# Sums of squares for queries and keys as two rounded passes, with the rotary products later in VectorE's order

## What is computed

```python
h = rms_norm(x, norm_w[i])
proj = jnp.einsum('bld,dn->bln', h, w_in)
# A: 4 heads of 128 with two softmax maps each, B: 4 query and 2 key heads,
# C: 4 latent heads (low-rank query and key), D: pooling; each times SiLU(gate)
q = rms_norm(q_raw, q_norm_w)      # over 64 or 128 numbers of a head
k = rms_norm(k_raw, k_norm_w)
q, k = rotate(q), rotate(k)        # part of A's, all of B's, 64 of C's
p = softmax(q @ k.T * scale)
y = p @ v
x = x + concat(A, B, C, D) @ w_out[i]
```

## Time and profile before

| | |
|---|---|
| median of three runs | 905.96 us (905.85 to 906.21) |
| the profiled execution | 905.9 us, its span 904.1 us |
| TensorE matmul busy | 896.1 us, 99% |
| VectorE busy | 639.3 us, 71% |
| ScalarE busy | 566.3 us, 63% |
| TensorE clock granted | 1.000 of full speed (2.4 GHz) |

### The profile page before, as it was taken

One profiled execution on the slowest core, in us unless ns is written; L12 is line 12 of the kernel. 1 busy time (PEld: TensorE's weight loads), 2 busy tenths in 40 slices (PEclk: granted clock), 3 DMA queues, 4 the chain that ended last, 5 costly groups with the idle time before them and its releaser, 6 DMA issues.

```text
span 904.1 us, 18068 instructions
## 1 busy us (share of the span) xinstructions
PE 896.1 (99%) x7070; PEld 860.1 (95%) x7070; DVE 639.3 (71%) x1073; ACT 566.3 (63%) x985; POOL 0.2 (0%) x4
## 2 busy tenths in 40 slices
PE   8999999999999999999999999999999999999998
PEld 7999998998999999999999999999999999999998
DVE  7785987779777776766665659876787667766552
ACT  7678756577666667745554588556676666665331
POOL 0000000000000000000000000000000000000000
PEclk9999999999999999999999999999999999999999
DMA  8754433333434343444455553344324444445562
GB/s 333 264 197 142 150 129 131 123 139 113 149 138 146 134 156 121 154 144 188 169 199 186 187 181 146 126 136 160 140 98 183 140 141 159 150 159 187 187 211 70
DMA packets 22996, 143.83 MB, mean 159 GB/s; under 512 B 2560, under 2 KB 4736, under 8 KB 6528
## 3 DMA queue, kind: packets, MB, share of 16 engines
q1 hardware_dynamic: 22768, 142.64, 43.7%
q10 hardware_dynamic: 144, 0.04, 0.0%
HBM read 140.58 MB, written 2.10 MB: 158 GB/s over the span
## 4 chain that ended last, share of the span: by engine, by line
PE 94%; ACT 3%; DVE 2%; DMA 1%; issue 0%; SPq 0%; ACTq 0%; DVEq 0%
PE dense L733 26%; PE dense L735 25%; PE dense L734 25%; PE s_ps L902 4%; PE o_ps L938 4%; PE norm_ps L857 2%; PE t_ps L917 2%; ACT w_hi L1028 1%; DVE w_lo L1331 1%; DMA x<-xt_dram 1%; PE swap_ps L881 0%; ACT h_hi L1009 0%; PE swap_ps L735 0%; PE norm_ps L735 0%; PE norm_ps L734 0%
## 5 line engine op out<-in xcount | busy, mean ns | idle before, releaser
L733 PE MATMUL dense<-h_hi,w_hi 128*128 128x272 f32 (+2 forms) x1440 | 427.2, 297 | 1.9 <-DVE h_lo L1311 1.8
L735 PE MATMUL dense<-h_hi,w_lo 128*128 128x272 f32 (+2 forms) x1440 | 412.8, 287 | 0.0
L734 PE MATMUL dense<-h_lo,w_hi 128*128 128x272 f32 (+2 forms) x1440 | 411.0, 285 | 0.0
L1331 DVE TENSOR_TENSOR w_lo<-raw,w_hi 128x1024 fp32r<-128x1024 f32 (+1 forms) x257 | 313.3, 1219 | 87.3 <-ACT w_hi L1028 80.5
L1028 ACT ACTIVATE w_hi<-raw 128x1024 fp32r<-128x1024 f32 (+1 forms) x257 | 271.4, 1056 | 70.8 <-PE dense L735 56.1
L733 PEld LDWEIGHTS dense<-h_hi,w_hi 128*128 128x128 f32 x1440 | 271.4, 188 | 7.4 <-issue 3.0
L734 PEld LDWEIGHTS dense<-h_lo,w_hi 128*128 128x128 f32 x1440 | 271.5, 189 | 1.2
L735 PEld LDWEIGHTS dense<-h_hi,w_lo 128*128 128x128 f32 x1440 | 271.2, 188 | 0.0
L733 PE MATMUL dense<-y_hi,w_hi 128*128 128x272 f32 (+1 forms) x500 | 143.6, 287 | 0.5 <-DVE w_lo L1331 0.3
L735 PE MATMUL dense<-y_hi,w_lo 128*128 128x272 f32 (+1 forms) x500 | 142.7, 285 | 0.0
L734 PE MATMUL dense<-y_lo,w_hi 128*128 128x272 f32 (+1 forms) x500 | 142.4, 285 | 0.0
(11 more groups left out here) (173 smaller groups left out, 805.7 us busy)
## 6 DMA issues: line engine op xcount, KB each, us to landing
raw<-w_stream_dram SPq DMA_DIRECT2D x128, 1024.0 KB, 4.8
out_dram<-x SPq DMA_DIRECT2D x8, 256.0 KB, 5.9
x<-xt_dram SPq DMA_DIRECT2D x3, 544.0 KB, 8.9
raw<-w_stream_dram SPq DMA_DIRECT2D x3, 512.0 KB, 7.6
con<-consts_dram SPq DMA_DIRECT2D x1, 984.0 KB, 8.2
x<-xt_dram SPq DMA_DIRECT2D x2, 272.0 KB, 4.8
raw<-w_stream_dram SPq DMA_DIRECT2D x2, 256.0 KB, 4.5
d_w<-consts_dram SPq DMA_DIRECT2D x2, 256.0 KB, 5.5
```

What stands on the lines that cost most here:

```text
L733: nc.tensor.matmul(ps, whi, xhi, start=first, stop=False)
L734: nc.tensor.matmul(ps, whi, xlo, start=False, stop=False)
L735: return nc.tensor.matmul(ps, wlo, xhi, start=False, stop=last)
L1331: signal(nc.vector.tensor_tensor(w_lo[:, g % RING, 0:n], raw[:, e % RAW, CHUNK * half:CHUNK * half + n], w_hi[:, g % RING, 0:n].bitcast(F3 ...
```

## The change

All 36 sums of squares of queries and keys are made by two passes of fp32r operands instead of one product of float32 operands. The squares are split into a high part `sq_hi` and a low part `sq_lo`. For a single tile ScalarE writes the high part with a rounding copy after the square, and a new stage `sq_low` on VectorE subtracts. For a pair VectorE makes both behind the addition in `sq_sum`: a copy and a subtraction. The ones are rounded once into `sums_of` on ScalarE. The single tiles' rotary products become the stage `rope_turn` at 0.65 of their slot instead of 0.25, so behind `s_scale`, `rescale` and `s_max` and ahead of `rope_fin`, the gate and the split; b's pairs keep `rope_mid` at 0.25. For aq and ak the sum and the finish come one slot later, and `sub_slot` excludes slots 5 and 6 of a pair instead of 4 and 5.

```diff
--- before.py
+++ after.py
@@ -129,7 +129,7 @@
 AT_SCALAR = dict(rope_fin=-0.166, lat_fin=0.07, mix_out=0.09, lat_pre=0.097, sub_fin=0.1, rope_pre=0.11,
                  y_split=0.66, xscale=0.283, sub_pre=0.439, x_out=0.55, p_out=0.56, gate=0.65, s_exp=0.579,
                  lift=0.6, up_out=0.705, up_next=0.715, split=0.71, x_square=0.72, y_gate=0.73, y_lat=0.74, lam_exp=0.793, v_out=1.297)
-AT_VECTOR = dict(sq_sum=0.2, rope_mid=0.25, s_max=-0.418, lam_dot=-0.35, sub_fin=-0.345, rope_fin=-0.34, lat_fin=0.055, head_out=0.17,
+AT_VECTOR = dict(sq_sum=0.2, sq_low=0.6, rope_mid=0.25, rope_turn=0.65, s_max=-0.418, lam_dot=-0.35, sub_fin=-0.345, rope_fin=-0.34, lat_fin=0.055, head_out=0.17,
                  y_split=0.75, pool=0.266, xscale=0.283, gate=0.7, s_scale=0.491, x_out=0.512, rescale=0.55,
                  x_add=0.614, split=0.71, lam_out=0.82, y_gate=0.76, y_lat=0.72)
 
@@ -178,9 +178,10 @@
                 s = end + 1 + j
                 if kind in ("aq", "ak"):
                     at(s, ("rope_pre", l, kind, i0 + j, j))
-                    at(s, ("rope_mid", l, kind, i0 + j))
-                    at(s, ("rope_stat", l, kind, i0 + j))
-                    at(s + 1, ("rope_fin", l, kind, i0 + j))
+                    at(s, ("rope_turn", l, kind, i0 + j))
+                    at(s, ("sq_low", "rope", l, kind, i0 + j))
+                    at(s + 1, ("rope_stat", l, kind, i0 + j))
+                    at(s + 2, ("rope_fin", l, kind, i0 + j))
                 elif kind in ("bq", "bk"):
                     if j == 0:
                         at(s, ("rope_pre", l, kind, i0 // 2, None))
@@ -209,7 +210,8 @@
             at(s + n + 2, ("lat_fin", l, key))
             at(s + 2 + 2 * n, ("y_split", "lat_fin", l, key))
         at(s + 9, ("rope_pre", l, "kr", 0, None))
-        at(s + 10, ("rope_mid", l, "kr", 0))
+        at(s + 9, ("sq_low", "rope", l, "kr", 0))
+        at(s + 10, ("rope_turn", l, "kr", 0))
         at(s + 10, ("rope_stat", l, "kr", 0))
         at(s + 11, ("rope_fin", l, "kr", 0))
 
@@ -223,7 +225,8 @@
             if key in PAIRED:
                 at(s, ("sq_sum", "rope", l, key, i))
             else:
-                at(s + 1, ("rope_mid", l, key, i))
+                at(s, ("sq_low", "rope", l, key, i))
+                at(s + 1, ("rope_turn", l, key, i))
             at(s + 1, ("rope_stat", l, key, i))
             at(s + 2, ("rope_fin", l, key, i))
         last = len(query_tiles(l)) - 1
@@ -257,7 +260,7 @@
     taken = set()
     for p, (kind, _) in enumerate(PAIRS):
         if kind in ("aq", "ak", "bq", "bk"):
-            taken |= {pair_slot(p) + 4, pair_slot(p) + 5}
+            taken |= {pair_slot(p) + 5, pair_slot(p) + 6}
     while s - l * SLOTS in taken:
         s += 1
     return s
@@ -296,6 +299,9 @@
     c_st = sb("c_st", [128, 8, L])
     row = sb("row", [128, 2, L + 2 * PAD])
     sq = sb("sq", [128, 4, L])
+    sums_of = sb("sums_of", [128, 128], F32R)
+    sq_hi = sb("sq_hi", [128, 2, L], F32R)
+    sq_lo = sb("sq_lo", [128, 2, L], F32R)
     rn = sb("rn", [128, L])
     tab = sb("tab", [128, 2, L + 16])
     ta, tb = tab[:, 0, :], tab[:, 1, :]
...
@@ -849,13 +856,13 @@
 
         def rope_stat(l, key, i):
             t0 = rope_from(l, key)
-            if key in PAIRED:
-                pe.wait_ge(summed, sum_no[("rope", l, key, i)])
-            else:
-                pe.wait_ge(pre_done, pre_no[("rope_pre", l, key, i)])
+            pe.wait_ge(summed, sum_no[("rope", l, key, i)])
             norm_free("rope_stat", l, key, i)
-            sums = nc.tensor.matmul(norm_ps[:, t0:L], halves, sq[:, 2 * parity("rope_stat", l, key, i), t0:L],
-                                    start=True, stop=True)
+            half = parity("rope_stat", l, key, i)
+            if (l, key, i) == (0, "qn", 0):
+                    pe.wait_ge(ones_ready, 1)
+            nc.tensor.matmul(norm_ps[:, t0:L], sums_of[:, :], sq_hi[:, half, t0:L], start=True, stop=False)
+            sums = nc.tensor.matmul(norm_ps[:, t0:L], sums_of[:, :], sq_lo[:, half, t0:L], start=False, stop=True)
             sums.then_inc(stat_done, 1)
 
         def lat_stat(l, key):
@@ -997,6 +1004,8 @@
             act.wait_ge(lam_ready, 1)
             act.wait_ge(tails_zero, 1)
             signal(nc.scalar.activation(lam_sum[:, :], lam_sum[:, :], ACT.Exp), lam_exp, 1)
+            act.wait_ge(s_const, 16)
+            nc.scalar.activation(sums_of[:, :], halves, ACT.Copy).then_inc(ones_ready, 1)
 
         def x_tile(l, kt):
 
@@ -1097,7 +1106,8 @@
                 signal(nc.scalar.activation(sq[:, 2 * half:2 * half + 2, t0:L], pair_source(key, i)[:, :, t0:L],
                                             ACT.Square), pre_done, pre_no[("rope_pre", l, key, i)])
                 return
-            signal(nc.scalar.activation(sq[:, 2 * half, t0:L], rope_source(key, i)[:, t0:L], ACT.Square), pre_done,
+            link(nc.scalar.activation(sq[:, 2 * half, t0:L], rope_source(key, i)[:, t0:L], ACT.Square))
+            signal(nc.scalar.activation(sq_hi[:, half, t0:L], sq[:, 2 * half, t0:L], ACT.Copy), pre_done,
                    pre_no[("rope_pre", l, key, i)])
 
         def lat_pre(l, key):
@@ -1354,9 +1364,20 @@
             t0, half = rope_from(l, key), parity("rope_stat", l, key, i)
             dve.wait_ge(pre_done, pre_no[("rope_pre", l, key, i)])
             a, b = sq[:, 2 * half, t0:L], sq[:, 2 * half + 1, t0:L]
-            signal(nc.vector.tensor_tensor(a, a, b, ALU.add), summed, n)
-
-        def single_mid(l, key, i):
+            link(nc.vector.tensor_tensor(a, a, b, ALU.add))
+            high = sq_hi[:, half, t0:L]
+            link(nc.vector.tensor_copy(high, a))
+            signal(nc.vector.tensor_tensor(sq_lo[:, half, t0:L], a, high.bitcast(F32), ALU.subtract), summed, n)
+
+        def sq_low(what, l, key, i):
+
+            t0, half = rope_from(l, key), parity("rope_stat", l, key, i)
+            dve.wait_ge(pre_done, pre_no[("rope_pre", l, key, i)])
+            signal(nc.vector.tensor_tensor(sq_lo[:, half, t0:L], sq[:, 2 * half, t0:L],
+                                           sq_hi[:, half, t0:L].bitcast(F32), ALU.subtract), summed,
+                   sum_no[(what, l, key, i)])
+
+        def rope_turn(l, key, i):
 
             branch, t0 = rope[key][0], rope_from(l, key)
             src, out_ = (a(key, i)[:, t0:L] for a in (rope_source, rope_target))
@@ -1376,9 +1397,6 @@
             link(nc.vector.tensor_tensor(out_, out_, ta[:, t0:L], ALU.add))
 
         def rope_mid(l, key, i):
-            if key not in PAIRED:
-                single_mid(l, key, i)
-                return
             t0 = rope_from(l, key)
             n = L - t0
             out_, t = pair_target(key, i)[:, :, t0:L], tab[:, :, t0:L]
...
```

More of the change, by code:

```diff
@@ L395, in build @@
     lam_ready, lam_exp = sem("lam_ready"), sem("lam_exp")
+    ones_ready = sem("ones_ready")
     tails_zero = sem("tails_zero")
@@ L503, in build @@
             scaled_no[stg[1:]] = len(scaled_no) + 1
-        if stg[0] == "sq_sum":
+        if stg[0] in ("sq_sum", "sq_low"):
             sum_no[stg[1:]] = len(sum_no) + 1
-        if stg[0] == "rope_mid":
+        if stg[0] in ("rope_mid", "rope_turn"):
             mid_no[stg[1:]] = len(mid_no) + 1
@@ L1514, in _ @@
         run = dict(setup=setup, split_half=split_half, x_half=x_half, x_first=x_first, x_add=x_add, lam_dot=lam_dot, lam_out=lam_out,
-                   x_out=x_out, split=split, rescale=rescale, sq_sum=sq_sum, rope_mid=rope_mid, rope_fin=rope_fin,
+                   x_out=x_out, split=split, rescale=rescale, sq_sum=sq_sum, sq_low=sq_low, rope_mid=rope_mid, rope_turn=rope_turn, rope_fin=rope_fin,
                    lat_fin=lat_fin, sub_fin=sub_fin, head_out=head_out, y_split=y_split, gate=gate, pool=pool,
@@ L1519, in _ @@
         for stage, *what in vector_plan:
-            if stage in ("rope_mid", "rope_fin") and not waited[0]:
+            if stage in ("rope_mid", "rope_turn", "rope_fin") and not waited[0]:
                 dve.wait_ge(s_tab, 16)
```

## The result

The changed kernel takes 914.08 us in the median of 5 runs (912.43 to 914.39), against 905.96 us before: a ratio of 1.0083, 95% interval 1.0072 to 1.0095. It is 8.1 us slower. The forecast was 906.5 us with a range to 909.5, so the time lies outside it, on the slow side. The profiled execution took 914.16 us (span 912.2).

What follows compares the result with a forecast made beforehand. TensorE was taken as the bound, with VectorE a second one in its full stretches. Losses of 7.9 us against 7.3 saved gave +0.6 us on 905.96, so 906.5 us, with a range from 901.0 to 909.5.

Steps and rivals of the forecast that it cites:

- What bounds the kernel: Whole kernel: TensorE, busy 896.1 of 904.1 us; VectorE a second bound in the latent stretches and at 204 to 235 us.
- What TensorE saves: All 36 sums: two rounded passes take 0.252 or 0.237 us instead of 0.46 or 0.43, saving 7.3 us at most.
- The prices on the other engines: Work added for the sums: 21.9 us on VectorE and 10.1 us on ScalarE, at 442, 304 and 431 ns per operation.
- Latent heads: Up to chunk 28: added VectorE work delays its low half, losing 2.3 us in layer 0 and 2.4 in layer 1.
- Other steps have over 1.5 us of slack and cost nothing: Steps not given a loss of their own: over 1.5 us of slack, so no loss.
- Head a: Slots 53 to 61: late softmax weights lose 1.7 us in layer 0; 0.6 us come back in layer 1.
- The 0.6 us: Head a of layer 1: TensorE's idle time before 674.83 us, claimed to come back through the new order.
- Head b: Pairs' added work loses 0.7 us at bq2 of layer 0, 0.6 at bk and 0.8 at bq0 of layer 1.
- (1): VectorE's gaps absorb all losses but the latent stretches': 903.4 us, or 901 if half of these are absorbed; chance 0.23.
- (2): Nearly the whole TensorE saving arrives, with no stall in the latent stretches: 898.7 to 900 us; chance 0.10.
- (3): Latent stretches: late sums delay ScalarE's root, then VectorE's finish and low halves, 1.4 us more per layer: 909.3 us; chance 0.24.
- (4): Sums: a rounded pass at 128 ones goes at the old price (0.23), no saving and all losses: 913 us; chance 0.03.

Runs made afterwards that it cites:

- experiment 1: Kernel before, old order, sums as two rounded passes with the low part always zero and no added work: 900.53 us, ratio 0.994.
- experiment 7: Changed kernel with the latent heads' sums (kr, qr, qn, kn) in float32 as before, the others rounded: 906.55 us, ratio 1.0011.
- experiment 3: Kernel before with only the new order, sums in float32 and no new operations: 905.75 us, ratio 0.9996.
- experiment 10: Changed kernel with all its work, but sums wait only for the high part and the second pass reads zeros: 912.32 us, ratio 1.0071.
- experiment 11: Changed kernel with only the single tiles' sums rounded, their subtractions on GpSimd, pairs as one float32 product: 906.01 us, ratio 1.0.
- experiment 5: Changed kernel with only the 22 single tiles' sums rounded, pairs as one float32 product without added work: 907.37 us, ratio 1.0022.

## Why the prediction was wrong

**What bounds the kernel: right, and not carried far enough.** It named VectorE a second bound in the latent stretches and at 204 to 235 us, which holds. It didn't read the stretch behind chunk 28, where VectorE was at 21.09 of 22.75 us.

**What TensorE saves: right.** 0.25 us a sum (experiment 1) against 0.252. But "the most that the passes can give" was then used in full: with all else unchanged 5.4 of 7.3 us arrive, and with the added work in place 3.2. (The table books the whole 7.3 and puts what does not arrive among the losses, so this is the same miss seen from the other side.)

**The prices on the other engines: right.** 442, 302 and 432 ns; VectorE grew by 20.0 us of busy time (21.9 was forecast with the gaps, and about 661 us in all; it is 659.3). The 202 ns worked out from the Trainium skill ("VectorE: DVE Perf Modes", the TRN2 errata section and the perf-mode tier table) are not borne out: 302 ns for this copy, which also rounds, and 304 for the plain one. The same page says under its table that the formula gives too little for a single operation.

**Latent heads: right up to chunk 28.** Chunk 28 of layer 0 started at 97.98 against 96.45, 1.53 us later, forecast "about 1.5 us later"; losses 2.4 and 2.7 us against 2.3 and 2.4. The low part of kn0 was forecast for about 87.4, and the sum that waited for it came at 87.62. Most of the lateness shows at the sums: at chunk 28 the first pass starts only some 0.2 and 0.3 us later than its predecessor allows (97.67 to 97.98, 559.68 to 560.09). In layer 1 the wait of 0.67 us for ScalarE's root of kr comes before these, and the working doesn't have it.

**The step that failed** is that the latent heads' term ends at chunk 28. It counts kr, qn0, kn0 and qr0; qr1, qn1 and kn1 behind them have no term in the sum, and with them slots 29 to 53, under "Other steps have over 1.5 us of slack and cost nothing". I had counted VectorE's lateness as paid once chunk 28 had waited for it. In truth that wait only brings TensorE level with a full queue. qr1, qn1 and kn1 bring 0.475 and twice 0.815 us into slots that are full too. TensorE runs on weights whose low halves are made three chunks ahead, but nothing is made ahead of the softmax weights, the pooled rows and the head's output, and it waited for these at 574.22, 578.62 and 584.82. Slots 29 to 53 lost 1.2 and 2.8 us in place of none. Experiment 7 shows that the latent heads' work is the cause of 3.4 of these 3.9 us. The chain from 561.79 us shows that in layer 1 VectorE's queue is the way; in layer 0 ScalarE's is a part of it.

**Head a: right in layer 0 but for the clock (3.4 - 1.7 = 1.7), which the prediction didn't have at all, and wrong in layer 1.** The clock isn't what put the time out of the range: at full clock it is 912.5 us, 3.0 above 909.5. The 0.6 us come back if only the order changes (experiment 3), but with the added subtractions the weights are late again, at 673.71, and the value product at 677.59: +0.5 instead of -0.6.

**Head b: right**, 0.7 us in layer 0 and 1.3 in layer 1 against 0.7 and 1.4.

**The rivals.** (1) and (2), with faster times, fell by the result. (3), slower by a feedback through ScalarE's root, had the right sign and not the mechanism: experiment 10 takes the sums' wait away and the time stays. ScalarE does have a part, but through its own copies: the wait at 545.62 for its root, and experiment 11. (4) fell in experiment 1. The misses add up: slots 29 to 53 3.9 us, the clock 1.7, head a of layer 1 1.1, the latent stretches 0.5, all else 0.3: 7.5 = 15.4 - 7.9.

Left open: how the 1.2 and 2.8 us of slots 29 to 53 divide between VectorE's and ScalarE's added work, as no run gave ScalarE's copies alone (VectorE's work for the pairs alone made 0.7 and 1.6); and what decides in which executions the clock falls.

## What to carry to other kernels

Where a queue is full, follow added work to the first slot in which the engine stands idle again, and ask of every operation in between who waits for it, not only of the large ones that the other engine leads with. Savings on one engine and added work on another don't add: price the work with the faster engine already waiting (here 3.2 us of a 7.3 us saving was left), and try the two halves alone. An average of 71% busy says nothing about a stretch at 93%.

## What the runs showed of the hardware

- **The clock behind a wait.** In the profiled execution of the changed kernel TensorE was granted 0.57 of its clock from 236 to 240 us, right behind a wait of 1.53 us; passes of 272 columns there start 0.227 us apart (236.25, 236.48, 236.70, 236.93) instead of 0.126. That is 1.7 us lost for a wait of 1.5. It is no fixed consequence: a wait of 1.52 us was followed by a granted clock of 0.50 in experiment 7 (at 232.62, the clock from 234 to 236) and of 1.00 in experiment 5 (at 232.85), one of 1.81 us in experiment 10 (at 234.83) by 1.00, and one kernel's executions differ in it.
- **GpSimd beside VectorE.** A subtraction of 272 columns takes 964 ns there (442 on VectorE), and a low half of VectorE that runs beside it 1464 ns instead of 1225 (14 of them), 1429 in experiment 11 (16 of them).
